# First layer's norms from rows of every eighth token, the gate copied out earlier, q and k turned one step on, in a two-layer hybrid block on one Trainium2 core

## What is computed

```python
h = rms_norm(x, norm_g)                      # x * rsqrt(mean(x*x) + eps) * g, per token
proj = h @ w_in                              # 1024 -> 4 branches, gates, merge gates
(q, k, v, z_a, p_in, z_b, u, v_sgu, z_c, glu_a, glu_b, z_d, merge) = jnp.split(proj, ...)
q = apply_rope(rms_norm(q, q_norm_g), cos, sin)      # 8 heads of 64
k = apply_rope(rms_norm(k, k_norm_g), cos, sin)      # 2 heads of 64
o_a = window_attention(q, k, v, sinks)
o_c = spatial_gating(u, v_sgu, ...)          # layer_norm(v_sgu), mixed over 128 positions, times u
```

## Time and profile before

| | |
|---|---|
| time, median of 3 runs | 2113.51 us (2112.78 to 2114.54) |
| the profiled execution | 2111.53 us |
| its span, first to last instruction | 2109.7 us |
| TensorE matmul busy | 2080.0 us, 99% |
| VectorE / GpSimd / ScalarE busy | 60% / 58% / 40% |
| mean granted TensorE clock | 0.994 of 2.4 GHz |
| chain that ended last, share of TensorE | 92% |
| DMA | 192.01 MB, mean 91 GB/s |

### The profile page before, as it was taken

How to read it: one execution, slowest core, us unless ns; L and a number is a source line. 1 busy time by engine, 2 the same in 40 slices (tenths; PEclk the granted TensorE clock), 3 DMA queues, 4 the chain that set the end, 5 groups by cost and what they waited for, 6 DMA issues and landing times.

```text
span 2109.7 us, 27162 instructions
## 1 busy us (share of the span) xinstructions
PE 2080.0 (99%) x9760; PEld 1720.5 (82%) x9760; DVE 1261.5 (60%) x1529; ACT 843.3 (40%) x1617; POOL 1228.9 (58%) x940
## 2 busy tenths in 40 slices
PE   9799999999999999999999999999999999999999
PEld 7697877788888888888888878778888888888887
DVE  3876544588878745335347865447888786452331
ACT  5533644334233335324436245443332343443331
POOL 2346544676659767654433565447767696675543
PEclk9899999999999999999999999999999999999999
DMA  7112232312441334314531123323134313434163
GB/s 265 41 35 85 66 115 85 120 51 67 85 94 46 76 84 81 135 55 155 165 102 50 31 87 96 102 74 112 60 75 89 73 51 82 89 70 140 51 200 100
DMA packets 112325, 192.01 MB, mean 91 GB/s; under 512 B 13888, under 2 KB 23360, under 8 KB 112192
## 3 DMA queue, kind: packets, MB, share of 16 engines
q1 hardware_dynamic: 93120, 159.00, 23.9%
q0 software_dynamic: 9216, 16.78, 5.9%
q10 hardware_dynamic: 9856, 14.50, 1.9%
HBM read 148.28 MB, written 41.95 MB: 90 GB/s over the span
## 4 chain that ended last, share of the span: by engine, by line
PE 92%; POOL 2%; DVE 2%; DMA 1%; ACT 1%; issue 1%; SPq 0%; DVEq 0%; POOLq 0%; ACTq 0%
PE acc L662 79%; PE aux L723 5%; PE acc L723 3%; POOL wlo L593 1%; PE aux L795 1%; PE aux L814 1%; PE aux L805 1%; POOL wsum L597 1%; PE aux L829 1%; DVE x L1393 1%; DMA rd<-rms 1%; PE aux L771 0%; DMA xrow<-x_rows 0%; DMA x<-x 0%; PE aux L757 0%
## 5 line engine op out<-in xcount | busy, mean ns | idle before, releaser
L593 POOL TENSOR_TENSOR wlo<-raw,whi 128x512 fp32r<-128x512 f32 x424 | 579.0, 1367 | 609.7 <-ACT whi L919 608.8
L662 PE MATMUL acc<-fhi,whi 128*128 128x512 f32 x2048 | 802.7, 392 | 3.4 <-DVE acc L1393 2.1
L662 PE MATMUL acc<-fhi,wlo 128*128 128x512 f32 x2048 | 797.7, 389 | 0.0
L662 PE MATMUL acc<-flo,whi 128*128 128x512 f32 x2048 | 797.5, 389 | 0.0
L919 ACT ACTIVATE whi<-raw 128x512 fp32r<-128x512 f32 x424 | 265.7, 627 | 490.3 <-PE acc L662 406.2
L662 PEld LDWEIGHTS acc<-fhi,whi 128*128 128x128 f32 x2048 | 385.1, 188 | 86.6 <-issue 6.3
L662 PEld LDWEIGHTS acc<-fhi,wlo 128*128 128x128 f32 x2048 | 384.8, 188 | 80.4
L662 PEld LDWEIGHTS acc<-flo,whi 128*128 128x128 f32 x2048 | 385.1, 188 | 78.3
L593 POOL TENSOR_TENSOR wlo<-wsum,whi 128x512 fp32r<-128x512 f32 x192 | 273.2, 1423 | 175.5 <-ACT whi L919 175.2
L1393 DVE SCALAR_TENSOR_TENSOR aux<-conv,allp,aux 128x1024 f32<-128x1024 f32 x232 | 299.1, 1289 | 19.6
L662 PE MATMUL acc<-bhi,whi 128*128 128x512 f32 x512 | 201.6, 394 | 0.0
(11 more groups left out here) (194 smaller groups left out, 2300.4 us busy)
## 6 DMA issues: line engine op xcount, KB each, us to landing
raw<-wstream SPq DMA_DIRECT2D x424, 256.0 KB, 2.7
md<-prev POOLq DMA_DIRECT2D x64, 256.0 KB, 4.2
x<-x SPq DMA_DIRECT2D x32, 256.0 KB, 5.6
md<-prev SPq DMA_DIRECT2D x32, 256.0 KB, 3.4
out<-x ACTq DMA_DIRECT2D x32, 256.0 KB, 2.2
mx<-md SPq DMA_DIRECT2D x24, 256.0 KB, 5.0
xrow<-x_rows SPq DMA_DIRECT2D x8, 512.0 KB, 7.9
qd<-qst ACTq DMA_DIRECT2D x16, 256.0 KB, 2.2
```

Of the source, the lines that this page charges most:

```text
L593: nc.gpsimd.tensor_tensor(wlo[:, f % SLOTS, :], src, whi[:, f % SLOTS, :].bitcast(F32), ALU.subtract).then_inc(lo_made, 1)
L662: mm = nc.tensor.matmul(dst, w, m[:, kt0 + k, cols], start=first and k == 0 and n == 0, stop=last and k == UK - 1 and n == 2, skip_group_c ...
```

## The change

It has four edits.

1. The row tiles take every eighth token (`x_rows.rearrange("(p t) d -> t p d", t=TT)[t]`), so that partition p has the sums of tokens 8p to 8p+7, and the store of the first layer's norms writes 128 pieces of 32 bytes. The rows are asked for and squared earlier (k = 1, 2, 3), and root, reciprocal and store come after k = 3. SyncE, not ScalarE, loads `spreads`, after a wait for the store at k = 5, and right behind it loads the norms back in the old layout (`rms`, 1024 elements of 4 bytes), ahead of x's tiles 6 and 7 and all that follows. VectorE waits for this (`rms_turned`) before it scales the variances.
2. The first loads are x's block (0, 1), the weights' unit 0, the columns and then x's block (0, 0); ScalarE splits unit 0 before it rounds x; `VS` starts on the four token tiles of t = 1 alone and waits for t = 0 at its fifth.
3. In the first layer ScalarE copies the gate's banks out after h's tile 4; h's tiles 5, 6 and 7 are rounded behind the copies.
4. In both layers `turn_q` 3 moves from ZC 0's p5 to its p2, `turn_k` from ZC 0's p2 to ZC 1's p1, the copies with them; and VectorE does `sum_22` of U 0 before `last_mixes`.

```diff
+        ROWS_AT = ((), (0, 1, 2), (3, 4, 5), (6, 7), (), (), (), ())
         def x_turn(L, k, t):
             if L == 0:
-                return 2 * k + t
+                return 2 * k + 1 - t
...
             def load_x(k):
+                for t in (1, 0):
+                    sp.dma_start(x_block(k, t), x[k * P:(k + 1) * P, t * HALF:(t + 1) * HALF]
+                                 ).then_inc(x_first if (k, t) == (0, 1) else x_loaded[k], 16)
+                    if (k, t) == (0, 1):
+                        load_unit(0, "VS", 0)
                         sp.dma_start(allp[:], cols).then_inc(cols_loaded, 16)
-                load_unit(0, "VS", k)
+                if k:
+                    load_unit(0, "VS", k)
...
-                sp.dma_start(xrow[:, t % 4, :], x_rows[t * P:(t + 1) * P, :]).then_inc(row_loaded[t % 4], 16)
-            for k, tiles in enumerate(((), (0,), (1, 2), (3, 4), (5, 6), (7,), (), ())):
+                sp.dma_start(xrow[:, t % 4, :], x_rows.rearrange("(p t) d -> t p d", t=TT)[t]
+                             ).then_inc(row_loaded[t % 4], 16)
+            for k in range(KT):
                 load_x(k)
-                for t in tiles:
+                for t in ROWS_AT[k]:
                     load_row(t)
+                if k == 5:
+                    sp.wait_ge(norms_stored, 16)
+                    sp.dma_start(spreads[:], rd[0:1].rearrange("o t p -> o (t p)").partition_broadcast(P)
+                                 ).then_inc(spread_loaded, 16)
+                    sp.dma_start(rms[:], rd[0].rearrange("t p -> p t"), allow_slow_non_contiguous=True
+                                 ).then_inc(rms_turned, 16)
...
+                        if name == "VS" and n_tile == 4:
+                            pe.wait_ge(x_ready, x_turn(L, k, 0) + 1)
...
-                pair(L, "ZC", 0, {"p6": lambda L=L: turn_q(L, 2), "p5": lambda L=L: turn_q(L, 3),
-                                  "p2": lambda L=L: turn_k(L)})
-                pair(L, "ZC", 1)
+                pair(L, "ZC", 0, {"p6": lambda L=L: turn_q(L, 2), "p2": lambda L=L: turn_q(L, 3)})
+                pair(L, "ZC", 1, {"p1": lambda L=L: turn_k(L)})
...
+                    act.dma_start(rd[L].rearrange("a (b t) -> (a b) t", t=TT), rms[:]).then_inc(norms_stored, 16)
...
+            high(0)
             act.wait_ge(cols_loaded, 16)
+            act.wait_ge(x_first, 16)
+            x_rounded(0, 0, 1)
+            act.wait_ge(x_loaded[0], 16)
+            x_rounded(0, 0, 0)
+            for k in range(1, KT):
                 act.wait_ge(x_loaded[k], 16 * 2)
...
-                if k == 5:
+                if k == 3:
                     rms_stage(0)
-                if k == 6:
                     store_norms(0)
...
                 else:
-                    load_spread(L)
                     next_high(L, "VS", 4)
-                    for k in range(5):
-                        h_rounded(L, k)
+                    h_rounded(L, 0)
+                    h_rounded(L, 1)
                 next_high(L, "VS", 5)
-                h_rounded(L, 5)
+                for k in (5,) if L else (2, 3):
+                    h_rounded(L, k)
                 next_high(L, "VS", 6)
-                h_rounded(L, 6)
+                h_rounded(L, 6 if L else 4)
                 act.wait_ge(half_done, 2 * L + 1)
                 take_vs(L, 4)
...
                 take_vs(L, 2)
+                if L == 0:
+                    next_high(L, "VS", 7)
+                    h_rounded(L, 5)
+                    h_rounded(L, 6)
                 h_rounded(L, 7)
...
-                gate_pair(L, "ZC", 1, branch_c, {"p1": lambda L=L: stage_keys(L, 0)})
+                                                 "p2": lambda L=L: take_turned_q(L, 3)})
+                gate_pair(L, "ZC", 1, branch_c, {"p1": lambda L=L: take_turned_k(L),
+                                                 "p6": lambda L=L: stage_keys(L, 0)})
...
+                if L == 0:
+                    dve.wait_ge(rms_turned, 16)
...
+                    sum_22(L, "U", i, BANK_AP["b"])
+                    dve.drain()
                     if i == 0:
                         last_mixes()
-                    sum_22(L, "U", i, BANK_AP["b"])
-                    dve.drain()
+                        dve.drain()
```

More of the change, by code:

```diff
@@ L265, in hybrid_block @@
         x_loaded = [sem(f"x_loaded{i}") for i in range(KT)]
+        x_first = sem("x_first")
+        rms_turned = sem("rms_turned")
         row_loaded = [sem(f"row_loaded{i}") for i in range(4)]
@@ L467, in load_x @@
             def load_x(k):
-                for t in range(2):
-                    sp.dma_start(x_block(k, t), x[k * P:(k + 1) * P, t * HALF:(t + 1) * HALF]).then_inc(x_loaded[k], 16)
-                    if (k, t) == (0, 0):
+                for t in (1, 0):
[3 more added lines that the diff above has]
+                        load_unit(0, "VS", 0)
                         sp.dma_start(allp[:], cols).then_inc(cols_loaded, 16)
-                load_unit(0, "VS", k)
+                if k:
+                    load_unit(0, "VS", k)
             def load_row(t):
@@ L977, in store_norms @@
                 act.wait_ge(norms_made, L + 1)
-                act.dma_start(rd[L].rearrange("t p -> p t"), rms[:], allow_slow_non_contiguous=True).then_inc(norms_stored, 16)
+                if L:
+                    act.dma_start(rd[L].rearrange("t p -> p t"), rms[:], allow_slow_non_contiguous=True
+                                  ).then_inc(norms_stored, 16)
+                else:
+                    act.dma_start(rd[L].rearrange("a (b t) -> (a b) t", t=TT), rms[:]).then_inc(norms_stored, 16)
             def load_spread(L):
@@ L1179, in _ @@
             nc.scalar.activation(nsink[:, 0:1], epst[:], ACT.Sqrt)
+            high(0)
             act.wait_ge(cols_loaded, 16)
-            for k, tiles in enumerate(((), (0,), (1, 2), (3, 4), (5, 6), (7,), (), ())):
+            act.wait_ge(x_first, 16)
[3 more added lines that the diff above has]
+            for k in range(1, KT):
                 act.wait_ge(x_loaded[k], 16 * 2)
-                for t in range(2):
-                    x_rounded(0, k, t)
+                x_rounded(0, k, 1)
+                x_rounded(0, k, 0)
                 if k < SLOTS:
@@ L1226, in _ @@
                 take_vs(L, 2)
+                if L == 0:
+                    next_high(L, "VS", 7)
+                    h_rounded(L, 5)
+                    h_rounded(L, 6)
                 h_rounded(L, 7)
-                next_high(L, "VS", 7)
+                if L:
+                    next_high(L, "VS", 7)
                 next_high(L, "Q", 0)
@@ L1736, in _ @@
             for k in range(KT):
-                if k == 7:
+                if k == 4:
                     norms(0)
-                for t in range(2):
+                for t in (1, 0):
                     x_rest(0, k, t)
```

2 lines of the change are left out of this document (removed).

## The result

The changed kernel took 2089.69 us (median of 4 runs, 2089.1 to 2090.13), the kernel before beside it 2113.15 (4 runs, 2112.11 to 2114.54). The ratio is 0.9888, with a 95% interval of 0.9871 to 0.9906: 23.5 us less, or 1.1%. The forecast was 2085.0, with a range of 2080.5 to 2098.0; 28.6 us were expected, so 5.1 did not come. The profiled execution took 2089.10 us with a span of 2087.3, 22.4 less than the span before.

The account below looks back on a forecast made before the run. TensorE computes for 2080 of 2109.7 us, so only its waits and the low clock behind them can go. 16.3 (opening) + 10.2 (turns) + 2.1 (sum) = 28.6 us, giving 2085.0; own range 2081 to 2089, widened to 2080.5 to 2098.

Parts of the forecast that it names:

- The store: Norms' store at the opening: issued at 25.6, landing after 3.5 us (bounds 2.2 and 11.36), so norms stored at 29.1.
- The turned read: Norms read back ahead of x's tiles 6 and 7: taken at 2 us, bounds 0 and 11.36; called the weakest step.
- The rival that gave it 11.36: Turned read costs what the old store did, `Q` at about 61.5, time 2094.6; chance 0.19.
- SyncE's queue: Loads in order behind the store's landing: 2.75 MB, 6.7 us at 0.408 MB per us, plus 0.7 to start.
- The start of the pass: VectorE's pass over h follows the landing of the gate's weights: 38.5, say 39, for 46.6 before.
- The tenth scaling: The scaling ahead of the gate's copies ends 11.0 us after the pass begins, plus 2 for two slowed by GpSimd.
- The clock: At `Q`, remaining wait 1.5 us (0 to 4); the old low-clock loss of 3.17 us counted as gained.
- 16.3: Gain at the opening, 66.39 + 3.17 − 53.3 us, counted to the absolute start of `Q`, the earlier start included.
- The start (edit 2): First `VS` matmul at 8.2 for 10.23, 2.0 us sooner, and 1.8 us of low clock back; both inside the 16.3.
- The turns: `turn_q` 3 in both layers: waits of 7.1 us and low clock of 3.1 vanish, 10.2 together, with 2.0 of cover.
- The rival of another wait: The turn finds another wait, so up to 10.2 us stays: 2095; chance 0.10.
- `sum_22` ahead of the mix: In U 0, bank d is freed 2.5 us earlier, taking away a wait of 1.03 us in each layer: 2.1.

Follow-up runs that it names:

- small_store: The changed kernel with the rows in the old form, so the norms' store writes 1024 pieces of 4 bytes and no turned read is needed: 2096.54 us.
- read_last: The changed kernel with the turned read issued last, behind the identity, the rows and the gate's weights: 2088.88 us.
- before_copies: The kernel before with only the gate's copies moved behind h's tile 1, the roundings of tiles 2 to 6 behind them: 2104.24 us.
- start_back: The changed kernel with the first loads, the roundings and the order within `VS` as in the kernel before: 2089.29 us.
- copies_first: The changed kernel with h's tiles 3 and 4 too rounded behind the gate's copies, which so stand behind tile 2: 2084.81 us.
- lag_all: copies_first and mix_last together, first-layer `h_rest` five blocks behind `h_scale` instead of two, turned read behind the tables, 19 warming products for 22: 2080.56 us.
- sum_back: The changed kernel with the last mixes before `sum_22` of U 0 again: 2089.36 us.
- mix_last: The changed kernel with `last_mixes` moved behind the last product with U in U 0: 2086.9 us.
- turns_back: The changed kernel with `turn_q` 3 and `turn_k` and their copies at their old places: 2101.0 us.

## Why the prediction was right or wrong

The sign and the two main mechanisms were right. The time lay in the stated range, but only because that was widened to 2098 for two rivals that both failed to come: the forecast's own range ended at 2089, 0.7 below it. Two of its signs failed too: the wait for `vs_taken` was over 4 us, and behind the store the loads fell to 157 GB/s. What was missed are terms at the opening and a mechanism at `sum_22`.

By spans 22.4 us went. TensorE's instructions behind the opening, up to `turn_q` 0 of U 1, come 11.45 us earlier (66.39 + 3.17 before, 56.35 + 1.76 after; `turn_q` 0 at 175.56 before and 164.11 after). The turns add 5.4 in the first layer (in MC 0 TensorE stands at 231.67 before where it has 214.81 after) and 5.1 in the second, U 0's sum nothing in either; 0.4 is not assigned. Against the forecast of 28.6 that is 4.85 less at the opening and 2.1 less at the sum, 0.3 more at the turns. By medians the gain is 23.5, 1.0 more, since the profiled executions are 1.6 and 0.6 below the medians of their four runs.

**The store: right, and better than taken.** Issue at 25.28 for 25.6, landing after 2.34 for 3.5. small_store shows that the form of the pieces did it.

**The turned read: right mechanism, cheaper.** Taken at 2, it held up the pass by 0.58 us at most (read_last). The rival that gave it 11.36 falls. The argument, that the slow part of the old store was writing DRAM, fits what small_store shows: the packets were done 6.3 us before the landing, and a read of as many pieces has no such tail. That it is the writing, and not something else about a store, was not tested by itself.

**SyncE's queue: the end right by luck, through errors that cancel.** The gate's weights landed at 39.1 where 38.5 to 39 was forecast. The store's landing was 1.5 us sooner and the read cost 1.4 or more less. But the DMA engines had run dry while SyncE waited for the store, and every DMA takes SyncE some 0.5 us to issue (five from 28.48 to 31.01, four blocks of x and a unit), so in 27.6 to 33.0 only 157 GB/s moved, where the forecast reckoned with 408 from 0.7 us on.

**The start of the pass: 1.55 late (40.55 for 39).** The step that failed is that the landing of the gate's weights ends the wait. When they landed, VectorE was not waiting: it had finished the rests of x's tile 7 at 38.97, whose last block landed at 36.44, and stood in a small instruction on 8 columns (`nsink`) that ended at 40.15. A memset of 0.27 us follows, and then the pass. The sum had set both small instructions to nothing. In the kernel before the first took 0.17 us, at 34.03, with no GpSimd instruction beside it and 12 us ahead of the pass; here it took 1.25 (1.18 of them in the chain) beside one of GpSimd's.

**The tenth scaling: 1.03 late.** It ended at 54.58, 14.03 after the first began, for 13. Three scalings were slow beside GpSimd, not two. The copies behind it took 1.77 for 1.3.

**The clock: 1.76 not counted.** With `Q` forecast to wait 1.5 us, full clock was assumed. The wait was 4.7, by the terms above and by `VS` having ended even a little sooner (51.65 for 51.8), and behind it the clock was at 1.2 GHz for 3.25 us. 1.55 + 1.03 + 0.47 + 1.76 = 4.8, and this is the whole of the opening's shortfall, 16.3 − 11.45: the path and the copies had been taken too short, and the clock at nothing. The prediction's own bound, a wait of at most 4 us if the pass starts at 42, was too narrow by the missing terms.

**The start (edit 2): right in its numbers, in part by luck, and wrong as part of a gain.** `VS` began at 7.88 at full clock, as said. But the 10.23 and the 1.8 us of low clock that it was held against belong to one execution: with the same order of the first loads `VS` began at 9.63 in before_copies and at 8.57 in start_back, at full clock, and with the new order it began between 7.60 and 8.63 in the kernels with 22 warming products. With the old order the start goes with the landing of unit 0, 5.3, 5.0 and 4.0 us after its issue. Since the copies end the wait ahead of `Q`, nothing of it reached the time (start_back). In the 16.3 this was no error, for it was counted to the absolute start of `Q`; but in a list of what each edit is worth it stands at zero. It is worth something only where `Q` doesn't wait, as in copies_first and lag_all; how much was not measured.

**The place of the copies (edit 3): 4.6 us**, the largest single part of the opening beside the store's 6.9. The change puts the copies behind h's tile 4 and the prediction weighed that place only; behind tile 2 they give another 4.9 (copies_first).

**The turns: right.** Forecast 10.2 with 2.0 us of cover, measured 10.5. The chain of the kernel after:

```profile
177.65 8.18 PE acc L678 x36
185.83 0.87 PE aux L789 x8
186.71 8.18 PE acc L678 x36
194.89 0.87 PE aux L797 x8
```

VectorE's last rotation ended at 183.89 (183.47 and 0.42 long), TensorE came to `turn_q` 3 at 185.83: 1.9 of cover, no wait, and no low clock behind it. The rival of another wait falls. None came ahead of MC 0 either.

**`sum_22` ahead of the mix: wrong.** The step that failed is the sentence "what moves behind it, the mix, is wanted only by the product with U, whose own end is unchanged". The mix's own reader is unhurt. But VectorE works in order, and behind the mix stand the rotation and the product that frees bank a. The wait for bank d had hidden a wait for bank a of nearly the same length: 2.1 us became 2.4, sum_back's waits turn the names back, and TensorE reaches U 1's `turn_q` 0 no sooner. mix_last shows that it was the order and not VectorE's load, since with the mix out of the way both waits vanish.

The prediction had set two sentences of the Trainium skill against its numbers, from "DMA: Bandwidth & Descriptors" (Rules for kernel authors and Specifications). That a strided last dimension lowers to one descriptor per element agrees with the packets: 1040 for the old form of the store, 144 for the new. That such a form is slow holds for the store (8.4 to 13.8 us) and not for the read of as many elements, 1.3 us behind its predecessor. And the 32-byte pieces, far under the page's 512 bytes, did not make the store slow, at 2.34.

## What to carry to other kernels

When an engine's wait shrinks, follow each instruction that stands between the last landing and the release, small ones and those beside a contending engine too, and ask which wait of the same length stands right behind the one that is removed: here the list of TensorE's waits showed it, once for `oc` and once ahead of `KV`. A step moved back in an in-order engine is paid by everybody who waits for what stands behind it, not by its own reader alone. And where a wait of a few us is followed by a clock that is low in one execution and full in the next, remove the wait altogether before weighing edits of one or two us.

## What the hardware showed that was not expected

*A store of 4 KB in 4-byte pieces costs 8.4 to 13.8 us, a read of the same pieces hardly anything.* 9.4 in the second layer, 11.36 before, 8.4 in small_store, 13.79 in before_copies, where 355 GB/s of loads ran beside it at first. In pieces of 32 bytes it is 2.34. The time is not in the packets: in small_store the last one began before 27.3 us and the landing came at 33.57, and a load of 256 KB whose packets were done too landed at 32.74, 12.0 us after its issue. The read held the path up by 0.58 us at most (read_last).

*VectorE's instruction ends only after GpSimd's beside it has ended.* On GpSimd and on VectorE of the kernel after (start us, us, line, operation):

```profile
46.27 1.69 POOL L609 TENSOR_TENSOR wlo<-raw,whi 128x512 fp32r<-128x512 f32 x1 [3.15 <-ACT whi L936]
```

```profile
46.72 1.78 DVE L1423 SCALAR_TENSOR_TENSOR x<-x,allp,spreads 128x512 f32<-128x512 f32 x1
```

GpSimd's ended at 47.96, VectorE's at 48.50, 0.54 later, and alone such a scaling takes 0.74. The instruction on 8 columns began at 38.90 and ended at 40.15, GpSimd's beside it at 40.13. The Trainium skill, in "SBUF — State Buffer" (Who interferes with whom), says that a VectorE instruction with two inputs in SBUF and a GpSimd instruction that reads SBUF exclude each other for a whole instruction; the scaling's times agree. The instruction on 8 columns reads only one tensor, so that sentence does not cover it; it took 0.17 us in the kernel before, 1.25 here, and 1.26 in before_copies, where it ended at 35.22 and GpSimd's beside it at 35.20.

*The low clock behind a wait of 3.5 to 9.1 us has no fixed price.* The first 12 matmuls of `Q`, 2.72 us at 2.4 GHz, took 3.00 behind a wait of 3.5 us, 4.36 behind 3.9, 4.48 behind 4.7, 5.26 behind 6.0 (small_store) and 4.34 behind 9.1. In turns_back, of two waits of 3.56 us in one execution, the first had full clock behind it and the second not; and one and the same kernel (sum_back) came out at 2087.5 or at 2091.3.
